# A one-layer hybrid trunk: the output projection of tile 6 spread over the last tile's inverse levels, a split last projection, and router logits from unnormalised rows

## The chip, the cores and the metric

One Trainium2 chip, one core, one launch. Times are microseconds (us) on the device for that core; one execution was also recorded by the hardware profiler. Everything is float32.

## What is computed

For 1024 tokens of width 1024, cut to what matters here:

```python
h = rms_norm(x, attn_norm_g);  proj = h @ w_in            # 1024 x 2824
y_a = gated_delta_rule(...)    # 4 heads of 128; a chunk of 64 needs the inverse of (I + strict lower)
y_a = rms_norm(o_a, gdn_out_norm_g) * silu(a_z)
y_b = swa_sink_attention(...)  # 8 heads of 64, own and previous chunk, a sink logit per head
x = x + concat([y_a, y_b]) @ w_out
tok = rms_norm(x, ffn_norm_g)
gl = tok @ w_group + b_group   # 4 groups, top 1;  el = tok @ w_expert + b_expert, top 2 of 4 experts
for e in range(16):
    gu = tok @ w_gate_up[e];  act = silu(gu[:, :256]) * gu[:, 256:]
    y = y + gates[:, e:e+1] * (act @ w_down[e])
x = x + y
```

## The kernel before

Each engine has its own program, written out by hand: PE (TensorE, matmuls and transposes), ACT (ScalarE, copies out of PSUM and exponentials), DVE (VectorE), POOL (GpSimd), SP (only starts DMAs). Semaphores join them. Each engine takes its instructions in the order of its program, so a wait holds all that stands behind it.

**First part, eight tiles of 128 tokens.** `run_tiles` calls `body(t, nx, pv, nn)` for tiles 0 to 7. Beside tile t's own recurrence and attention, the body projects tile t+1 (`nx`), finishes tile t-1 (`pv`, the "late" work) and scales and turns tile t+2 (`nn`). In the last tile, 7, `nx` is None, so the 2824-column projection that fills PE elsewhere is not there. After it `late(7)` finishes tile 7.

A body has a loop over six inverse levels. In each, PE multiplies into bank 3 (`X,aTm`), ACT copies that to `Y`, PE multiplies `Y` and the running inverse into banks 2 and 5, and DVE subtracts the results from `X` and `aTm` (the lines `L1253`, `L1261`). `xT0_ready` is the DVE's start of that chain (`L1237`).

The late work of a tile is: turn `y_mix` (PE), copy to `pT` (ACT), multiply by `wo_sb` in two halves of 512 columns (`out_half`, 8 slices k each, accumulated in one bank), add the rows of x (`add_x`, `L1162`, into `sc`, also called `xr`), square and sum (ACT), the reciprocal root in 12 small steps (`rsqrt`, `L940` to `L946`), scale to `y_mix` (`L1168`), which is also stored as `h_mid`, turn the scaled rows (`turn_hm`), copy with the gain (`L1174`, `hT2`), multiply by the router matrix (`w_rt`), add the bias (`L1179`, `lg`).

**Routing.** From `lg`, DVE finds groups and experts (`route_picks`), PE counts ranks, DVE gives each token a slot and makes one-hot rows (`row_hots`, `L1014`, `L1015`; `gate_hot`, `L1019`), PE sums them into tables in banks 0 (rows) and 3 (gates). For tiles 0 to 5 this is done ahead: `picks_ahead` in the last body, `rows_ahead` in `late(7)`. Tiles 6 and 7 follow after the last logits. `rows_ready` lets POOL gather.

**Second part, 32 expert steps.** Expert e has a first slot set (even step) and a second (odd step), each up to 128 rows, gathered from `h_mid` and scattered to `out` by POOL. Before the first step PE loads 17 flags into registers (`second`, `spilled`); an odd step's matmuls are skipped when its flag is 0. Weights stream through four ring slots, of which three lie in the memory of `w_in`, and the fourth in that of `w_out`.

## Time and profile before

| | us |
|---|---|
| three runs | 1098.81, 1102.18, 1107.79 |
| median | 1102.18 |
| profiled execution, its own time | 1106.72 |
| span that the profile shows of it | 1104.5 |
| mean granted TensorE clock of it | 0.942 |

The span runs from the first to the last recorded instruction, so 2.2 us of the profiled execution lie outside it. That execution is 4.5 us above the median, within what the three runs differ by. Every start time below counts from the start of the span. PE is recorded as busy for 90% of the span.

### The profile page before, as it was taken

The page shows a single profiled execution, that of the slowest core. Times are in us where ns is not written, and L with a number is a line of the kernel's source. Part 1 is how long each engine was busy: PE and PEld are TensorE (multiplying, and loading weights), DVE is VectorE, ACT ScalarE, POOL GpSimd, SP SyncE. Part 2 cuts the span into 40 slices and gives each one's busy share as a digit, 9 for nine tenths or more (in the row PEclk, how much of TensorE's full clock was granted, in tenths as well). Part 3 has the DMA queues.
Part 4 walks back from the last instruction along what each step waited for, and adds up shares of the span by engine and source line. Part 5 has one row for each costly group of instructions (what it writes and reads, how often), then busy time and mean ns, then how long its engine had stood idle before and what let it go on. Part 6 is the DMA issues. An engine that isn't in the chain of part 4 may idle for free.

```text
span 1104.5 us, 17185 instructions
## 1 busy us (share of the span) xinstructions
PE 997.0 (90%) x6912; PEld 690.0 (62%) x6912; DVE 591.3 (54%) x1768; ACT 215.3 (19%) x453; POOL 156.2 (14%) x227
## 2 busy tenths in 40 slices
PE   6999999999999999999999967874698998987994
PEld 2456656656656656656666655744677786866873
DVE  1446756757665675674684675575124333333332
ACT  1333233223223222321331330100000000000000
POOL 6010010010010010010010020001123223333231
PEclk9989999999999999999999978886799999989997
DMA  9700101100100100000000002804157777767321
GB/s 319 301 19 2 39 1 40 39 1 39 39 1 39 39 1 39 22 18 39 20 1 39 20 1 75 326 15 162 61 191 279 261 250 251 270 231 275 100 63 40
DMA packets 48521, 109.57 MB, mean 99 GB/s; under 512 B 10289, under 2 KB 11569, under 8 KB 48433
## 3 DMA queue, kind: packets, MB, share of 16 engines
q1 hardware_dynamic: 32880, 82.87, 21.1%
q0 software_dynamic: 13824, 25.20, 6.9%
q8 instruction: 63, 1.03, 0.4%
q10 hardware_dynamic: 1728, 0.26, 0.1%
q14 instruction: 26, 0.20, 0.1%
HBM read 108.30 MB, written 25.17 MB: 121 GB/s over the span
## 4 chain that ended last, share of the span: by engine, by line
PE 80%; DVE 10%; DMA 4%; issue 4%; ACT 1%; POOL 0%; POOLq 0%; ACTq 0%; DVEq 0%
PE pm L341 73%; PE pm L344 7%; DMA qkvT<-h_mid,w_sb 2%; DMA y_mix<-h_mid,w_sb 1%; DVE X L1253 1%; DMA sc<-h_mid,w_sb 1%; DVE y_mix L1168 0%; DVE ctmp L1230 0%; ACT ci L754 0%; DVE qkT L1241 0%; DVE aTm L1203 0%; DVE bs L946 0%; DVE bs L944 0%; DVE bs L945 0%; DMA xt<-in_x 0%
## 5 line engine op out<-in xcount | busy, mean ns | idle before, releaser
L341 PE MATMUL pm<-w_sb,hT 128*128 128x512 f32 (+1 forms) x768 | 315.8, 567 | 2.9 <-DVE hT L1074 2.8
L341 PEld LDWEIGHTS pm<-w_sb,hT 128*128 128x128 f32 x768 | 145.3, 193 | 153.5 <-issue 145.1
L341 PE MATMUL pm<-wo_sb,pT 128*128 128x512 f32 x256 | 120.7, 627 | 1.2 <-ACT pT L811 1.2
L341 PE MATMUL pm<-ctmp,w_sb 128*128 128x128 f32 x768 | 90.7, 280 | 0.0
L341 PEld LDWEIGHTS pm<-ctmp,w_sb 128*128 128x128 f32 x768 | 89.5, 197 | 0.0
L1116 DVE SCALAR_TENSOR_TENSOR pqkv<-ci,cw,pqkv 128x128 f32<-128x128 f32 x288 | 77.7, 346 | 20.5 <-ACT pqkv L759 20.0
L341 PEld LDWEIGHTS pm<-wo_sb,pT 128*128 128x128 f32 x256 | 50.3, 202 | 60.5 <-issue 58.9
L1515 POOL TENSOR_TENSOR tail<-tail,rows 128x512 f32<-128x512 f32 x8 | 10.2, 1276 | 489.1 <-ACT aTm L778 489.1
L915 ACT ACTIVATE X<-pm 128x256 f32<-128x256 f32 x32 | 12.3, 384 | 315.3 <-PE pm L341 292.4
L341 PE MATMUL pm<-w_sb,Y 128*128 128x512 f32 x152 | 70.2, 605 | 2.9 <-DVE Y L1423 2.9
L1253 DVE TENSOR_TENSOR X<-X,pm 128x256 f32<-128x256 f32 (+1 forms) x40 | 16.8, 419 | 75.3 <-PE pm L341 75.3
L344 PE MATMUL pm<-ident,y_mix 128*128 128x128 f32 x192 | 29.0, 301 | 25.3 <-DVE y_mix L1333 14.2
L341 PE MATMUL pm<-ci,w_sb 128*128 128x128 f32 x448 | 51.2, 275 | 0.0
L341 PEld LDWEIGHTS pm<-ci,w_sb 128*128 128x128 f32 x448 | 50.6, 192 | 0.0
L341 PEld LDWEIGHTS pm<-w_sb,Y 128*128 128x128 f32 x152 | 28.0, 195 | 31.2 <-issue 31.2
L1162 DVE TENSOR_TENSOR sc<-sc,pm 128x512 f32<-128x512 f32 x16 | 11.0, 688 | 66.1 <-PE pm L341 66.1
L344 PEld LDWEIGHTS pm<-ident,y_mix 128*128 128x128 f32 x192 | 24.4, 156 | 31.6 <-DVE y_mix L1333 14.5
L1433 DVE SCALAR_TENSOR_TENSOR xt<-pm,w_sb,xt 128x512 f32<-128x512 f32 x16 | 11.6, 749 | 50.6 <-PE pm L341 50.6
L1433 DVE SCALAR_TENSOR_TENSOR pqkv<-pm,w_sb,pqkv 128x512 f32<-128x512 f32 x16 | 11.6, 748 | 45.4 <-PE pm L341 45.4
L845 ACT ACTIVATE Y<-pm 128x256 f32<-128x256 f32 (+1 forms) x48 | 18.3, 382 | 86.9 <-PE pm L341 86.9
L344 PE MATMUL pm<-ident,qkvT 128*128 128x128 f32 x128 | 18.6, 293 | 18.3 <-issue 10.0
L1433 DVE SCALAR_TENSOR_TENSOR tail<-pm,w_sb,tail 128x512 f32<-128x512 f32 x16 | 12.0, 751 | 40.6 <-PE pm L341 40.6
(273 smaller groups left out, 1502.3 us busy)
## 6 DMA issues: line engine op xcount, KB each, us to landing
w_sb<-in_w_gate_up SPq DMA_DIRECT2D x12, 2048.0 KB, 10.2
w_sb<-in_w_down SPq DMA_DIRECT2D x12, 1024.0 KB, 5.9
w_sb<-in_w_in SPq DMA_DIRECT2D x5, 2048.0 KB, 17.3
wo_sb<-in_w_gate_up SPq DMA_DIRECT2D x4, 2048.0 KB, 11.2
xt<-in_x SPq DMA_DIRECT2D x8, 512.0 KB, 3.3
wo_sb<-in_w_out SPq DMA_DIRECT2D x1, 4096.0 KB, 23.1
sc<-in_x SPq DMA_DIRECT2D x8, 512.0 KB, 3.3
out<-sc SPq DMA_DIRECT2D x8, 512.0 KB, 2.6
```

The lines of the kernel that those rows point to most:

```text
L341: return pe.matmul(o_, lhsT=l_, rhs=r_, start=start, stop=stop, skip_group_check=True)
L344: return pe.transpose(o_, in_, ident[:, :])
L845: act.activation(Yd[rows_], heads(pm[3], CH)[rows_], ACT.Copy).then_inc(B.y_copied, 1)
L915: act.activation(tnh, pm[2 + p % 2][:, 0:DE], ACT.Tanh, scale=0.5).then_inc(M.tanh_ready, 1)
L1116: ins = v.scalar_tensor_tensor(cv[:, i, :], ci[:, i, j:j + P], cw[:, j, i:i + 1], cv[:, i, :], ALU.mult, ALU.add)
L1162: v.tensor_tensor(xr[:, 512 * n:512 * n + 512], xr[:, 512 * n:512 * n + 512], pm[6 + n][:, :], ALU.add).then_inc(B.xm_ready, 1)
L1253: v.tensor_tensor(Xd[rows_], Xd[rows_], heads(pm[2], CH)[rows_], ALU.subtract).then_inc(B.x_updated, 1)
L1433: ins = v.scalar_tensor_tensor(y[:, n * 512:n * 512 + 512], pm[4 + 2 * b + n][:, :], gate, y[:, n * 512:n * 512 + 512], ALU.mult, ALU.add)
L1515: g.tensor_tensor(qk_in[:, 0:QH, :], qk_in[:, 0:QH, :], gqk[:, None, 0:DH].broadcast_to([P, QH, DH]), ALU.mult)
```

## The change

Seven things are done to the program.

1. In tile 7 the late work of tile 6 is laid out over the levels. `out_half` takes a list of slices: five slices of the first half stand before level 0, three in level 0, four and four of the second half in levels 1 and 2, the turning in level 3, the logits in level 4. The results go to banks 0 and 1 instead of 6 and 7, and the attention scores of tile 7 go to `xt`, since `sc` now holds tile 6 longer. The 29 DVE instructions of `picks_ahead` are cut in four pieces, which with `add_x`, `copy_hT2`, `factor` and `scale_xm` are put behind the levels' own instructions. PE's `rank_ahead` moves behind level 5.
2. In `late(7)` the attention half of `y_mix` (slices 4 to 7) is turned and projected first, and the other half after `ya_ready`.
3. In every tile the logits are made from the unnormalised rows (`turn_xm` turns `xr`), and the row's factor is applied when the logits are copied (`scalar_tensor_tensor`). The scaled rows are still made for `h_mid`, on DVE, and in `late(7)` on ACT.
4. The last tile leaves out the update of the state `S`, which nothing reads.
5. The gates of all eight tiles are made after `rows_ready`: their 16 one-hot arrays (two picks by eight tiles) are built there one by one, where before twelve stood in `rows_ahead` and four behind `rows_ready`.
6. PE, and the other engines, load one register with all flags packed in its bits (`powers`), and an odd step tests its bit with a register operation. PE's first expert step waits for `rows_ready`, not `table_ready`.
7. SP issues the nine MB of the first three ring slots before the stores of tile 6.

```diff
+        def scores(t):
+            return sc_last if t == NT - 1 else sc
+
+        def late_banks(t):
+            return (pm[0], pm[1]) if t == NT - 2 else (pm[6], pm[7])
...
-                if pv is not None:
-                    store(pv)
...
+                if pv is not None:
+                    store(pv)
 
                 sp.wait_ge(B.p_turned, t + 1)
+                if nx is None:
+                    sp.wait_ge(L.mid_stored, 32 * t)
+                    sp.wait_ge(B.hm_turned, 2 * t)
...
+            def out_half(t, n, ks=range(KD), first=0, last=KD - 1):
+                for k in ks:
+                    ins = mm(late_banks(t)[n][:, :], yT[:, k, :], wo_sb[:, k, n * 512:(n + 1) * 512], k == first, k == last)
+                if ks[-1] == last:
+                    ins.then_inc(B.out_done, 1)
...
+            def turn_xm(t):
+
+                for n in range(2):
+                    pe.wait_ge(B.xm_ready, 2 * t + n + 1)
+                    for k in range(4):
+                        ins = turn(late_banks(t)[n][:, k * P:(k + 1) * P], xr[:, (4 * n + k) * P:(4 * n + k + 1) * P])
+                    ins.then_inc(B.hm_turned, 1)
...
-
-            def turn_hm(t):
-                pe.wait_ge(B.hm_ready, t + 1)
-                for k in range(KD):
-                    ins = turn(pm[6 + k // 4][:, (k % 4) * P:(k % 4 + 1) * P], y_mix[:, k * P:(k + 1) * P])
-                ins.then_inc(B.hm_turned, 1)
-
-            def logits(t):
-                pe.wait_ge(B.hT2_ready, 2 * t + 2)
...
+                    if k % 4 == 0:
+                        pe.wait_ge(B.hT2_ready, 2 * t + 1 + k // 4)
+                    ins = mm(late_banks(t)[0][:, 0:NL], hT2[:, k, :], w_rt[:, k, :], k == 0, k == KD - 1)
...
-                        mm(pm[3][:, 0:P], hot_mod[u], hot_gate[u], u == 0, False)
...
-                turn_y(t)
-                out_half(t, 0)
-                out_half(t, 1)
+                pe.wait_ge(B.yb_ready, t + 1)
+                for k in range(4, KD):
+                    ins = turn(pm[7][:, (k % 4) * P:(k % 4 + 1) * P], y_mix[:, k * P:(k + 1) * P])
+                ins.then_inc(B.y_turned, 1)
+                pe.wait_ge(B.yT_ready, t + 1)
+                for n in range(2):
+                    out_half(t, n, range(4, KD), 4, 3)
+                pe.wait_ge(B.ya_ready, t + 1)
+                for k in range(4):
+                    ins = turn(pm[2][:, k * P:(k + 1) * P], y_mix[:, k * P:(k + 1) * P])
+                ins.then_inc(B.y_turned, 1)
+                pe.wait_ge(B.yT_ready, t + 2)
+                for n in range(2):
+                    out_half(t, n, range(4), 4, 3)
+                turn_xm(t)
+                logits(t)
                 rows_ahead()
-                turn_hm(t)
-                logits(t)
...
+                if pv is not None and nx is not None:
+                    pe.wait_ge(B.yT_ready, pv + 1)
                     out_half(pv, 0)
...
+                if nx is None:
+                    pe.wait_ge(B.yT_ready, pv + 1)
+                    pe.wait_ge(F.chunk_copied, 6 * NT)
+                    out_half(pv, 0, range(0, 5))
+                elif pv is not None:
                     out_half(pv, 1)
                 ahead(2)
-                if nx is None:
-                    rank_ahead()
...
-                    turn_hm(pv)
+                if pv is not None and nx is not None:
+                    turn_xm(pv)
...
+                        if nx is None:
+                            out_half(pv, 0, range(5, KD))
+                        elif pv is not None:
                             logits(pv)
-                    elif l == 1 and nx is not None:
+                    if nx is None:
+                        if l == 1:
+                            out_half(pv, 1, range(0, 4))
+                        elif l == 2:
+                            out_half(pv, 1, range(4, KD))
+                        elif l == 3:
+                            turn_xm(pv)
+                        elif l == 4:
+                            logits(pv)
...
+                if nx is None:
+                    rank_ahead()
                 pe.wait_ge(B.v_ready, t + 1)
-                for h in range(H):
...
+                if nx is not None:
+                    for h in range(H):
+                        ins = mm(pm[5][:, h * P:(h + 1) * P], kd[:, h, :], V[:, h, :])
+                    ins.then_inc(B.s_done, 1)
...
-            pe.wait_ge(R.gate_hots, 1)
-            for u in late_hots:
-                ins = mm(pm[3][:, 0:P], hot_mod[u], hot_gate[u], False, u == late_hots[-1])
+            for u in range(TOPK * NT):
+                pe.wait_ge(R.gate_hots, u + 1)
+                ins = mm(pm[3][:, 0:P], hot_mod[u], hot_gate[u], u == 0, u == TOPK * NT - 1)
             ins.then_inc(R.gates_summed, 1)
...
-            second = [pe.value_load(full[0:1, e:e + 1], min_val=0, max_val=1) for e in range(NE)]
-            spilled = pe.value_load(full[0:1, NE:NE + 1], min_val=0, max_val=1)
+            spilled = pe.value_load(full[0:1, 0:1], min_val=0, max_val=2 ** (NE + 1) - 1)
...
-                with pe.If(second[ORDER[p // 2]] > 0):
+                e = ORDER[p // 2]
+                with pe.If(spilled % 2 ** (e + 1) > 2 ** e - 1):
...
-                    pe.wait_ge(R.table_ready, 1)
+                    pe.wait_ge(R.rows_ready, 1)
...
+                act.wait_ge(B.y_turned, t + 1)
+                act.activation(yT[:, 4:8, :], heads(pm[7]), ACT.Copy).then_inc(B.yT_ready, 1)
+                act.wait_ge(B.y_turned, t + 2)
+                act.activation(yT[:, 0:4, :], heads(pm[2]), ACT.Copy).then_inc(B.yT_ready, 1)
                 square_xm(t)
+                act.wait_ge(B.late_step, VL * NT)
+                act.activation(y_mix[:, :], xr, ACT.Copy, scale=bs[:, 89:90]).then_inc(B.hm_ready, 1)
...
-                v.wait_ge(A.exp_out, 1)
-                route_step(gates(0, AHEAD))
-                v.wait_ge(F.h_turned, NT)
-                v.wait_ge(F.chunk_done, 6 * NT)
                 for c in range(TOPK):
                     for t in range(AHEAD):
-                        row_hots(c, t)
-                        gate_hot(c, t).then_inc(A.hots, 1)
+                        row_hots(c, t).then_inc(A.hots, 1)
...
                     for b in range(2):
-                        v.tensor_tensor(hT2[:, 4 * b:4 * b + 4, :], heads(pm[6 + b]), wide(gain2[:, 4 * b:4 * b + 4]),
-                                        ALU.mult).then_inc(B.hT2_ready, 1)
+                        v.wait_ge(B.hm_turned, 2 * self.t + b + 1)
+                        v.tensor_tensor(hT2[:, 4 * b:4 * b + 4, :], heads(late_banks(self.t)[b]),
+                                        wide(gain2[:, 4 * b:4 * b + 4]), ALU.mult).then_inc(B.hT2_ready, 1)
...
-                    v.tensor_tensor(lg[:, bass.ds(self.t, 1), :], pm[6][:, 0:NL].unsqueeze(1), b_rt.unsqueeze(1),
-                                    ALU.add).then_inc(B.lg_ready, 1)
+                    v.scalar_tensor_tensor(lg[:, self.t, :], late_banks(self.t)[0][:, 0:NL], bs[:, 89:90], b_rt,
+                                           ALU.mult, ALU.add).then_inc(B.lg_ready, 1)
...
                 f.add_x(0)
                 f.add_x(1)
-                f.norm()
                 f.copy_hT2()
+                f.factor()
                 f.copy_logits()
...
-                if nx is None and nn is None and t == NT - 1:
-                    picks_ahead()
-                if pv:
+                if pv and nx:
                     pv.add_x(0)
                     pv.add_x(1)
...
-                    pv.norm()
+                if pv and nx:
                     pv.copy_hT2()
+                    pv.factor()
+                    pv.scale_xm()
...
+                    if not nx:
+                        if l == 1:
+                            pv.add_x(0)
+                            v.wait_ge(R.iotas, 1)
+                            route_groups(0, AHEAD)
+                        elif l == 2:
+                            pv.add_x(1)
+                        elif l == 3:
+                            pv.copy_hT2()
+                            route_first(0, AHEAD)
+                        elif l == 4:
+                            pv.factor()
+                            pv.scale_xm()
+                            route_second(0, AHEAD, A.exp_in)
+                        elif l == 5:
+                            pv.copy_logits()
+                            picks_ahead()
...
+                if nx:
+                    step(v.tensor_tensor(S[:, :, :], S[:, :, :], wide(cd), ALU.mult))
+                else:
+                    v.wait_ge(L.mid_stored, 32 * t)
...
+            tt(full_f, full_f, powers, ALU.mult)
+            step(v.tensor_reduce(gmax[:, 0:1], full_f, AX_X, ALU.add))
+            v.tensor_copy(full, gmax[:, 0:1]).then_inc(R.ready, 1)
+            v.wait_ge(R.ready, 1)
+            v.wait_ge(A.exp_out, 1)
+            v.wait_ge(R.exp_out, 1)
+            step(gates(0, NT))
+            for c in range(TOPK):
+                for t in range(NT):
+                    gate_hot(c, t).then_inc(R.gate_hots, 1)
...
+            for e in range(NE + 1):
+                step(g.memset(powers[:, e:e + 1], float(2 ** e)))
```

On PE, in the last tile from the end of its first small products to its first level, before:

```order
L341 MATMUL pm6<-wo_sb,pT 128x512 x8
L341 MATMUL pm3<-qkvT 128x128 x4
L341 MATMUL pm5<-qkvT 128x128 x4
L341 MATMUL pm7<-wo_sb,pT 128x512 x8
L341 MATMUL pm1<-w_sb,upper_strict 128x96
L341 MATMUL pm1<-w_sb,ones 128x96
L341 MATMUL pm2<-eye,aTm 64x64 x8
L344 MATMUL pm6<-ident,y_mix 128x128 x4
L344 MATMUL pm7<-ident,y_mix 128x128 x4
L341 MATMUL pm3<-X,aTm 64x64 x8
L341 MATMUL pm4<-S,qkvT 128x128 x4
L341 MATMUL pm6<-w_rt,pT 128x20 x8
```

And now (`wo_sb,pT` are slices of the output projection, `eye,aTm` turns the start of the inverse, `X,aTm` is level 0):

```order
L352 MATMUL pm3<-qkvT 128x128 x4
L352 MATMUL pm5<-qkvT 128x128 x4
L352 MATMUL pm0<-wo_sb,pT 128x512 x5
L352 MATMUL pm2<-eye,aTm 64x64 x8
L352 MATMUL pm3<-X,aTm 64x64 x8
L352 MATMUL pm4<-S,qkvT 128x128 x4
L352 MATMUL pm0<-wo_sb,pT 128x512 x3
L352 MATMUL pm2<-Y,aTm 64x64 x8
L352 MATMUL pm5<-aTm,Y 64x64 x8
L352 MATMUL pm3<-X,aTm 64x64 x8
L352 MATMUL pm1<-wo_sb,pT 128x512 x4
```

The first half's eight slices are cut in five and three, the second half begins in level 1, and the transposes, the logits and the two rank products have left this place.

On DVE, at the place where the inverse's start is made in the last tile, before (`lg` to `w_sb` is routing, the row `sc<-sc,pm6` is `add_x`, and three masked products follow it):

```order
L954 TENSOR_TENSOR w_sb<-w_sb 128x96 x2
L984 TENSOR_TENSOR w_sb<-w_sb 128x96
L1028 TENSOR_TENSOR w_sb<-w_sb 128x16 x6
L1162 TENSOR_TENSOR sc<-sc,pm6 128x512
L1162 TENSOR_TENSOR sc<-sc,pm7 128x512
L1230 TENSOR_TENSOR ctmp<-ctmp,bs 128x512
L1232 TENSOR_TENSOR Y<-pm3,ctmp 64x4x64
L1233 TENSOR_TENSOR ctmp<-pm3,ctmp 64x4x64
```

And now, where the mask of `dT` (`ctmp<-ctmp,upper`) is followed at once by the product with beta and the masked products:

```order
L1278 TENSOR_TENSOR ctmp<-ctmp,upper 128x512
L1282 TENSOR_TENSOR ctmp<-ctmp,bs 128x512
L1284 TENSOR_TENSOR Y<-pm3,ctmp 64x4x64
L1285 TENSOR_TENSOR ctmp<-pm3,ctmp 64x4x64
L1286 TENSOR_TENSOR ctmp<-pm3,ctmp 64x4x64
L1288 TENSOR_TENSOR aTm<-ctmp,level_mask 128x4x64
L1289 TENSOR_TENSOR aTm<-eye,aTm 128x4x64
```

The same engine in level 3 now has the two copies of the turned rows and part of the routing behind its own two subtractions:

```order
L1306 TENSOR_TENSOR X<-X,pm2 128x4x64
L1314 TENSOR_TENSOR aTm<-aTm,pm5 128x4x64
L1228 TENSOR_TENSOR pT<-pm0,gain2 128x512
L1228 TENSOR_TENSOR pT<-pm1,gain2 128x512
L1023 TENSOR_REDUCE w_sb<-w_sb 128x6
L1000 TENSOR_TENSOR w_sb<-w_sb 128x24 x2
L1005 TENSOR_REDUCE w_sb<-w_sb 128x6
L1000 TENSOR_TENSOR w_sb<-w_sb 128x24
```

On PE, in the late work of tile 7, before (the alternating one-hot products go on to twelve pairs, and only then come the turning and the logits):

```order
L344 MATMUL pm6<-ident,y_mix 128x128 x4
L344 MATMUL pm7<-ident,y_mix 128x128 x4
L341 MATMUL pm6<-wo_sb,pT 128x512 x8
L341 MATMUL pm7<-wo_sb,pT 128x512 x8
L341 MATMUL pm0<-pqkv,ci 128x128
L341 MATMUL pm3<-xt,ci 128x128
L341 MATMUL pm0<-pqkv,ci 128x128
L341 MATMUL pm3<-xt,ci 128x128
L341 MATMUL pm0<-pqkv,ci 128x128
L341 MATMUL pm3<-xt,ci 128x128
```

And now:

```order
L355 MATMUL pm7<-ident,y_mix 128x128 x4
L352 MATMUL pm6<-wo_sb,pT 128x512 x4
L352 MATMUL pm7<-wo_sb,pT 128x512 x4
L355 MATMUL pm2<-ident,y_mix 128x128 x4
L352 MATMUL pm6<-wo_sb,pT 128x512 x4
L352 MATMUL pm7<-wo_sb,pT 128x512 x4
L355 MATMUL pm6<-ident,sc 128x128 x4
L355 MATMUL pm7<-ident,sc 128x128 x4
L352 MATMUL pm6<-w_rt,pT 128x20 x8
L352 MATMUL pm0<-pqkv,ci 128x128 x10
```

The four-slice projection stands between the two turns of `y_mix`, and the one-hot products of tiles 0 to 5 stand behind the logits.

## Rows read from the trace of the kernel before

**Rows 1.** The page: the clock granted to TensorE, in tenths, in 40 slices.

```profile
PEclk9989999999999999999999978886799999989997
```

**Rows 2.** Waits of PE, 0 to 650 us: line waited for, sum, times, longest.

```profile
PE pm L344 <- DVE y_mix L1168: 2.5, 6, 0.4
```

**Rows 3.** Timeline of DVE, last tile: start, length, instruction, idle before.

```profile
664.78 0.18 DVE L967 TENSOR_REDUCE w_sb<-lg 128x6 f32<-128x24 f32 x1
...
671.20 0.68 DVE L1162 TENSOR_TENSOR sc<-sc,pm 128x512 f32<-128x512 f32 x1
...
676.41 0.69 DVE L1162 TENSOR_TENSOR sc<-sc,pm 128x512 f32<-128x512 f32 x1 [4.53 <-PE pm L341]
...
679.42 0.42 DVE L1237 TENSOR_TENSOR aTm<-eye,aTm 128x256 f32<-128x256 f32 x1
...
706.53 0.41 DVE L1253 TENSOR_TENSOR X<-X,pm 64x256 f32<-64x256 f32 x1 [1.60 <-PE pm L341]
...
713.99 0.69 DVE L1303 TENSOR_TENSOR V<-pm,bs 128x512 f32<-128x512 f32 x1 [1.75 <-PE pm L341]
...
715.82 0.76 DVE L1317 TENSOR_TENSOR y_mix<-pm,bs 128x256 f32<-128x256 f32 x2
...
723.08 0.69 DVE L1333 TENSOR_TENSOR y_mix<-X,gsz 128x512 f32<-128x512 f32 x1
```

**Rows 4.** Timeline of PE, last tile and late work.

```profile
658.39 9.33 PE L341 MATMUL pm<-wo_sb,pT 128*128 128x512 f32 x16
...
669.34 7.03 PE L341 MATMUL pm<-wo_sb,pT 128*128 128x512 f32 x16
...
684.26 1.97 PE L344 MATMUL pm<-ident,y_mix 128*128 128x128 f32 x8 [3.25 <-DVE y_mix L1168]
...
689.08 3.44 PE L341 MATMUL pm<-w_rt,pT 128*128 128x20 f32 x16
...
726.97 16.05 PE L341 MATMUL pm<-wo_sb,pT 128*128 128x512 f32 x32 [1.17 <-ACT pT L811]
```

**Rows 5.** Timeline of PE in tile 5, a level's product.

```profile
515.07 0.68 PE L341 MATMUL pm<-X,aTm 64*64 64x64 f32 x16
```

**Rows 6.** Timeline of DVE in the late work of tile 7.

```profile
723.69 0.25 DVE L954 TENSOR_TENSOR w_sb<-w_sb 128x96 f32<-128x96 f32 x1
...
728.22 0.28 DVE L1014 TENSOR_SCALAR ci<-w_sb 128x128 f32<-128x128 f32 x1
...
736.72 0.69 DVE L1162 TENSOR_TENSOR sc<-sc,pm 128x512 f32<-128x512 f32 x1
...
743.05 0.69 DVE L1162 TENSOR_TENSOR sc<-sc,pm 128x512 f32<-128x512 f32 x1 [5.64 <-PE pm L341]
...
749.28 1.29 DVE L1174 TENSOR_TENSOR pT<-pm,gain 128x512 f32<-128x512 f32 x2 [1.26 <-PE pm L344]
...
753.40 0.18 DVE L1179 TENSOR_TENSOR lg<-pm,rows 128x20 f32<-128x20 f32 x1 [2.83 <-PE pm L341]
```

**Rows 7.** Timeline of DVE, end of the routing.

```profile
761.95 0.29 DVE L1014 TENSOR_SCALAR ci<-w_sb 128x128 f32<-128x128 f32 x1
...
763.76 0.16 DVE L1050 TENSOR_REDUCE w_sb<-w_sb 128x2 f32<-128x8 f32 x1
...
766.86 0.18 DVE L1352 CAST w_sb<-w_sb 128x32 int32<-128x32 f32 x1
...
768.45 0.18 DVE L1377 CAST w_sb<-w_sb 128x17 int32<-128x17 f32 x1
```

**Rows 8.** Timeline of PE, the first expert step's transposes.

```profile
780.21 1.94 PE L344 MATMUL pm<-ident,qkvT 128*128 128x128 f32 x8 [10.02 <-issue]
```

**Rows 9.** The chain that ended last: start, length, what.

```profile
768.01 4.71 DMA qkvT<-h_mid,w_sb
```

**Rows 10.** Windows: length, PE, PEld, DVE, ACT, POOL busy (x), clock, DMA, GB/s.

```profile
688.00:690.00 2.00, 2.00 (x12) 2.00 (x11) 0.00 (x0) 0.00 (x0) 0.00 (x0) 0.50 0.99 332
728.00:730.00 2.00, 2.00 (x4) 0.97 (x3) 1.95 (x9) 0.00 (x0) 0.00 (x0) 0.50 0.00 0
```

122 lines of the change are left out of this document (57 added, 65 removed).

## The prediction

> **What bounds the kernel now.** The page comes first. TensorE holds nearly its full clock (2.4 GHz) nearly everywhere and loses it in one stretch, slices 24 to 29, which is 635 to 800 us [rows 1]. Before that place PE works almost without a gap, so what counts there is PE's own work; after it PE works through the experts with few waits. In between no engine is the bound: PE and DVE hand work to each other, and every microsecond of that chain moves the end. I therefore read the waits of PE before 650, then the timelines of DVE and PE from 650 to 790, then the granted clock in windows. All times below are on the axis of the profiled execution.
>
> **Tiles 1 to 6: minus 2.5 us.** In each of these bodies PE waits 0.4 us for the scaled rows, 2.5 in all [rows 2]. The turning now needs only `xr`, which is ready much earlier, so this goes. DVE does copies first and then 12 steps and the scaling. Between the turning and level 0's subtraction PE has, at full clock, a level's product 0.6 [rows 5], keys by state 1.05, the logits 1.8 (half of the 3.44 at half clock [rows 4]) and a second product 0.6, with the hand-over some 4.4 us; DVE's copies (1.29 [rows 6]), 12 steps (2.3) and scaling (0.75) take 4.35, so they just fit. The later store of `h_mid` is 4 us behind and nobody needs it for two levels. I count no cost, and up to 0.5 us a tile (3 us) for the bound.
>
> **Start of the inverse in tile 7: minus 12.2 us.** DVE is at 664.78 when it turns to the ahead routing, 6.4 us until 671.20; then it adds x for the first half, then waits 4.53 for PE's second half and adds at 676.41, and makes the inverse's start at 679.42, done at 679.84 [rows 3]. The masked products take from the end of the adding, 677.10, to there, 2.8 us. Without routing and adding they stand right behind 664.78: done at 667.6. Their inputs are early enough: the key products, which stood behind the first half of the projection, now come right at 658.4, where the first half began [rows 4], on the half clock, and end near 663. Five slices (ten of the sixteen passes of a half, 7.03 us at full clock [rows 4], so 4.4) fit into the rest. What is late next is this DVE chain itself, not PE.
>
> **The levels: about 0.** From the inverse's start to the subtraction of level 4 it is 679.84 to 706.53, 26.7 us [rows 3], with a 3.25 us wait for the scaled rows and then work on the half clock [rows 4, 10]. Now PE keeps its full clock, since it goes on working, but carries eleven more slices (22 passes of 0.44, 9.7 us). A product of the level is 0.6 us from start to start [rows 5]; three of them, DVE's subtraction and the hand-over, 0.5, stand in the chain. Level by level: turning and copying the start 1.2; level 0 with its product 0.6, keys by state 1.05, three slices 2.64, product 0.6, ends at 673.7; level 1 adds 0.5 + 0.6 + 3.5 + 0.6, 678.9; level 2 the same with 0.8 for the turns, 684.9; then scores and their maximum as before, 4.75 from level to level, 689.7, which hides the turning (1.04); level 4 has copies (1.3) and the logits' second half in the chain and takes 3.95, where the old one took 2.35. The subtraction of level 4 falls at 693.7, against 706.53: still 12.8 us ahead. DVE's inserted pieces are under PE's: adding and group routing (0.7 + 1.9) under the four slices of level 2, the first picks (1.1) under the logits.
>
> **The queues that are passed: 0.** On SP the weights of three ring slots now come before the stores of tile 6; they start when the last projection is done and have two levels' more time than the stores ask for, so nothing waits behind them; the x rows of tile 7 wait for those stores and are wanted only by the late work. POOL's 17 small fills stand before a signal that DVE needs only in level 1. If either were late, its price would be DVE's wait in the last tile, and I take none.
>
> **From level 4 to the logits of tile 7: minus 15.** Call the subtraction of level 4 T. Before, the logits are written at 753.58, T + 47.05 [rows 6]. Now, behind T: 1.3 for the inverse's own subtractions, factor 2.3, scaling 0.75, second picks 1.4, so level 5's product comes at T + 5.8 and its end at T + 6.9; the old order had T + 5.7. V's product needs PE's 1.1 and then `copy_logits` and the last picks (2.1) to pass: T + 9.1, against T + 7.46 [rows 3]. That is the price of this step, 1.6 us, and the missing state update pays 1.3 of it: the recurrence's half is in `y_mix` at T + 17.6 (was T + 17.24), the attention's half at T + 11.0. PE turns and copies that (1.3) and works 7.0 us on half of the projection, T + 19.3 at full clock; then turns the other half, copy 0.6, 7.0 more: T + 27.5. Before, the whole of it started at T + 20.4 and took 16.05 [rows 4], to T + 36.5. DVE meanwhile routes (3.7 + 12 pairs of arrays at 0.45, the rate of 761.95 to 763.76 [rows 7]; the triples ran from 728.22 to 736.72 [rows 6]) until T + 26.8, just ahead of PE. Adding ends at T + 28.2; then turning the second half 0.5, copying 0.7, logits 0.93 on one side, squares 1.25 and twelve steps 2.35 on the other: T + 32.1. The old chain took 743.74 to 753.58, 9.8 us [rows 6], the new one 3.9. Together 47.05 minus 32.1, 15.0.
>
> **The clock's surcharge: plus 2.** PE idled 7 us before the last projection, was then at 0.50 [rows 10], and 16.05 us went where 14.06 would do at full clock. Now it idles less but still has gaps from T + 4 to T + 12, so I expect the same surcharge of 2; the bounds are 0 and 7, the latter for all of the first half at 1.2 GHz. The Trainium skill (TensorE: Matmul & The Clock Gate, "Part 1: The HAM clock gate (the "warmup" mystery)") says that a model should leave the ramp out, as under 1% of a typical span. By that rule the sum would be 2 us better; the rows show the ramp as 2 us in this one place.
>
> **Routing tail: 0.** From the logits to `rows_ready` it is 753.58 to 767.04 [rows 6, 7], 13.5 us of the same instructions.
>
> **From there to the experts: minus 5.9.** Before, PE begins the first turn at 780.21, 13.2 us after `rows_ready`, after 10.02 without a releaser [rows 8]. The gather had landed at 772.72 [rows 9]. What stands in PE's program in that gap is 17 register loads, 0.59 each. Now: flags 0.66 as before plus 0.45, gates 0.8, 16 arrays at 0.25 are 4.1, last product 0.4, one load 0.6, hand-overs 0.3: 7.3. The gather needs 5.7 and is under it. POOL's first base gathers wait for the gates, 1.6 later than before, and are wanted over 20 us later. The Trainium skill (DMA: Bandwidth & Descriptors, "Latency and other measured facts") puts the floor of a `tensor_load` at some 600 ns; 17 of them give 10.2, and one load 0.6, so the sum stays, and its rule speaks against the rival that the stop is a fixed one.
>
> **Experts: 0.** Loads of the later weights follow PE's progress, the fourth ring slot is loaded 30 us before it is used, and PE's waits for gathers come from POOL's order of steps.
>
> **The sum.** 2.5 + 12.2 + 0.6 + 15.0 + 5.9 are 36.2, less 2 for the clock, 34. From the profiled execution's 1106.7 that is 1072.7; it stood 4.5 above the median of the runs, so against the median of 1102.2 it is 1068.
>
> **Rivals.**
> The stop before the experts is not the number of loads: then 10 us stay behind the gates instead of 0.6, and the gain falls by 9.4, to 1077. For it: no row names the loads. Against: nothing else is in the program there.
> DVE's pieces are not under PE's: if route pieces and late work add to every level (up to 8 us of the 12 put in) and PE drops to half clock in the first half (7 instead of 2), the gain is 21 to 28: 1074 to 1081. For it: levels 3 to 5 have little PE work; against: the pieces are shorter than the slices beside them.
> Nothing arrives: the experts' part ends when something of its own rhythm ends, and the gain dies there, 1092 to 1102. For it would be that PE waits several times for gathers; against, that these are sequential with the first step.
> Slower: the flag test. An odd step now makes a register operation with a remainder in PE's queue, 16 times, in front of a turn that the next copies wait for. By the nearest row, a register load of 0.59, it is 9.4 us, time 1077; it turns the sign when one costs over 2.1 us, and at 3 it gives 1116. No row shows such an operation; against a high price is only that it touches no memory.
> Better: the routing tail runs at full clock and the levels hide more, 1050 to 1058.
>
> **Chances.** The forecast 0.73 (its own range 1058 to 1078), the fixed stop 0.05, exposed pieces 0.12, nothing arrives 0.04, slower 0.03, better 0.03. What a measurement of this kernel can tell from no change is about 1%, 11 us. Faster by over 1% is all but the last part of "nothing arrives" and "slower": 0.93; within 1% 0.04; slower 0.03. The range from 1056 to 1083 takes in the forecast's bounds, the fixed stop and the exposed pieces.
>
> **What would show it.** In the profile after: the start of the inverse (`aTm<-eye,aTm`) some 12 us nearer to the masked `dT`, with no wait of DVE between; PE's clock at 1.0 through levels 0 to 2; the logits of tile 7 about 28 us earlier; at most 8 us from `rows_ready` to the first turn; PE's busy time in the experts' part unchanged. I am wrong if the gap before the first turn stays near 10 us, if the odd steps show an idle time that was not there, or if the levels in the last tile take clearly more than 27 us.

## Result and profile after

The changed kernel takes 1073.98 us (median of 4 runs, 1067.81 to 1075.96) against 1102.06 (4 runs, 1098.81 to 1107.79), a ratio of 0.9725, 95% interval 0.9687 to 0.9764. It was run twice more beside other kernels: 1072.85 (6 runs, ratio 0.9727, 0.9685 to 0.9769) and 1069.44 (6 runs, 0.9680, 0.9648 to 0.9711). The median of all 16 is 1072.55, which is 29.7 below 1102.2. The forecast was 1068, a gain of 34.

The first profiled execution of the changed kernel took 1075.61, span 1073.8. Its clock row, in slices of 26.8 us, answers to [rows 1]:

```profile
PEclk9999999999999999999999996986999998988998
```

Between 635 and 800 us three digits are below 9 (slices 25, 27 and 28) where six were. PE's waits up to 650 us (engine, output and line, what is waited for: us in total, times, longest):

```profile
PE pm L355 <- DVE xt L1118: 9.0, 1, 9.0
PE pm L352 <- DVE hT L1126: 2.8, 2, 1.4
PE pm L355 <- ACT ci L794: 2.4, 7, 0.3
PE pm L352 <- DVE V L1374: 0.8, 1, 0.8
```

The wait for the scaled rows [rows 2] is gone. Now DVE in the last tile (start, duration, engine, line, operation; it answers to [rows 3] and [rows 6]; `L1306` is the subtraction of level 4, the `L1214` row ends the last adding, `lg` are the logits of tile 7, and `CAST ... 128x32` is the end of `rows_ready`, as in [rows 7]):

```profile
667.13 0.68 DVE L1278 TENSOR_TENSOR ctmp<-ctmp,upper 128x512 f32<-128x512 f32 x1
670.25 0.42 DVE L1289 TENSOR_TENSOR aTm<-eye,aTm 128x256 f32<-128x256 f32 x1
...
697.45 0.41 DVE L1306 TENSOR_TENSOR X<-X,pm 64x256 f32<-64x256 f32 x1 [1.47 <-PE pm L352]
...
706.68 0.68 DVE L1374 TENSOR_TENSOR V<-pm,bs 128x512 f32<-128x512 f32 x1
714.62 0.69 DVE L1408 TENSOR_TENSOR y_mix<-X,gsz 128x512 f32<-128x512 f32 x1
...
725.35 0.69 DVE L1214 TENSOR_TENSOR sc<-sc,pm 128x512 f32<-128x512 f32 x1 [0.32 <-PE pm L352]
...
729.70 0.24 DVE L1233 SCALAR_TENSOR_TENSOR lg<-pm,bs,rows 128x20 f32<-128x20 f32 x1
...
743.15 0.18 DVE L1427 CAST w_sb<-w_sb 128x32 int32<-128x32 f32 x1
```

From the masked `dT` to the inverse's start it is 3.1 us, and DVE waits for nothing in between. From the end of the last adding to the logits it is 3.9 us (726.04 to 729.94), where it was 9.8 [rows 6]. PE, answering to [rows 4] and [rows 8]:

```profile
709.92 7.13 PE L352 MATMUL pm<-wo_sb,pT 128*128 128x512 f32 x16 [0.69 <-ACT pT L860]
718.18 7.13 PE L352 MATMUL pm<-wo_sb,pT 128*128 128x512 f32 x16 [0.69 <-ACT pT L862]
...
745.61 3.79 PE L352 MATMUL pm<-xt,ci 128*128 128x128 f32 x16 [3.26 <-DVE xt L1077]
749.19 1.91 PE L352 MATMUL pm<-hT,ci 128*128 128x128 f32 x8
750.89 1.20 PE L352 MATMUL pm<-hT,w_sb 128*128 128x128 f32 x8
751.93 1.04 PE L355 MATMUL pm<-ident,qkvT 128*128 128x128 f32 x8
```

Both halves of the last projection go at full clock, 7.13 us each. In front of the first turn (the last row) stand no longer 10 us without a releaser, but products: those of the 16 gate arrays, 745.61 to 752.09, the first of them at half clock (the granted clock from 743.3 to 752 was 0.55). The windows of the last tile (length, busy time of PE, PEld, DVE, ACT, POOL, granted clock, DMA share, GB/s):

```profile
646.00:664.00 18.00, 11.93 (x53) 11.11 (x54) 13.91 (x47) 6.34 (x11) 6.52 (x32) 0.50 0.97 368
664.00:697.00 33.00, 30.86 (x344) 20.73 (x345) 20.70 (x64) 5.64 (x14) 0.00 (x0) 0.97 0.05 18
697.00:703.00 6.00, 6.00 (x48) 5.66 (x47) 4.57 (x21) 1.47 (x3) 0.00 (x0) 0.50 0.01 1
703.00:734.00 31.00, 25.63 (x147) 16.16 (x145) 27.84 (x115) 3.98 (x7) 0.00 (x0) 0.99 0.22 73
```

The levels, which ran at half clock in part [rows 10], now have 0.97.

**One table for all runs.** Tiles 1 to 6 scatter from one execution to the next (below), so I cut each profiled execution at the same events. A: from the start to PE's turn of tile 7's rows (`ident,qkvT`, the first behind 640). B: to the inverse's start. C: to the subtraction of level 4. D: to the logits of tile 7. E: to the end of the row numbers' cast. F: to the first expert turn. G: to the end. "Lost" is the clock that was not granted between 60 and 640, the sum over windows of 2 us of 2 times (1 minus granted clock), which is worked out and no row. All in us.

```
kernel             A  (lost)    B     C     D     E     F      G    B to G   ratio
before          650.6 (6.1)   28.9  27.1  46.9  13.6  13.2  324.3   453.9
packed_only     648.0 (5.1)   29.9  24.8  45.3  13.6   5.9  325.1   444.6   0.9920
after           652.4 (11.1)  17.8  27.2  32.3  13.6   8.6  321.9   421.4   0.9725
control_after   646.0 (5.1)   17.8  27.7  32.3  13.0   8.4  321.5   420.6   0.9727
control_again   652.5 (11.1)  17.8  27.2  32.3  13.6   8.6  321.4   420.9   0.9680
loads17         646.0 (5.1)   17.8  27.7  32.3  13.0  17.2  326.3   434.3   0.9808
gates_in_gap    649.1 (8.5)   17.8  27.9  32.3  13.0   5.8  323.5   420.3   0.9680
whole_projection 646.7 (5.3)  17.8  27.1  42.8  13.6   8.6  321.6   431.4   0.9821
picks_first     645.8 (5.1)   24.2  28.8  30.5  13.6   8.5  321.8   427.4   0.9769
slices_first    646.7 (5.2)   17.8  28.7  32.3  13.0   8.3  321.5   421.5   0.9696
stores_first    648.8 (8.5)   16.6  27.2  41.9  13.1   7.6  320.4   426.7   0.9801
x_then_weights  646.7 (5.2)   17.8  27.1  32.3  13.6   8.7  321.6   421.1   0.9723
pieces_early    649.8 (8.0)   17.8  27.3  31.4  13.3   7.6  320.7   418.1   0.9667
pieces_gates    649.0 (8.5)   16.6  27.2  30.1  13.0   5.7  320.9   413.5   0.9678
```

The changed kernel's own three executions agree in B to G within 0.8 us, while A differs by 6.5. So a stage tells differences of about 1 us, while the three medians of this one program (4, 6 and 6 runs) differ by 4.5. But this was tried only on the changed kernel: the kernel before and `packed_only`, whose code is the same up to the end of E but for 17 small fills on POOL, differ by 1.0, 2.3 and 1.6 in B, C and D, with the clock.

### The profile page after: what moved, and what is told of

Read it like the earlier page. It is cut to its first block, busy times and chain, and to the rows that moved or that the text cites. A ratio compares the mean times of both kernels' runs of the same rounds, so it can differ in the third digit from the quotient of the medians.

```text
span 1073.8 us, 17149 instructions
## 1 busy us (share of the span) xinstructions
PE 993.0 (92%) x6904; PEld 686.4 (64%) x6904; DVE 588.6 (55%) x1763; ACT 216.7 (20%) x454; POOL 157.8 (15%) x244
## 4 chain that ended last, share of the span: by engine, by line
PE 84%; DVE 7%; DMA 5%; issue 2%; ACT 1%; POOL 0%; POOLq 0%; DVEq 0%; ACTq 0%
PE pm L352 77%; PE pm L355 6%; DMA qkvT<-h_mid,w_sb 2%; DMA y_mix<-h_mid,w_sb 1%; DVE X L1306 1%; DMA sc<-h_mid,w_sb 1%; ACT ci L794 0%; DVE w_sb L1000 0%; DMA xt<-in_x 0%; POOL out L1664 0%; DVE hT L1126 0%; DVE Y L1504 0%; DVE X L1502 0%; DVE tail L1514 0%; DVE bs L990 0%
## 5 line engine op out<-in xcount | busy, mean ns | idle before, releaser
L1306 DVE TENSOR_TENSOR X<-X,pm 128x256 f32<-128x256 f32 (+1 forms) x40 | 16.8, 419 | 63.6 <-PE pm L352 63.6
L1214 DVE TENSOR_TENSOR sc<-sc,pm 128x512 f32<-128x512 f32 x16 | 11.0, 686 | 59.7 <-PE pm L352 59.7
L788 ACT ACTIVATE tail<-pm 128x512 f32<-128x512 f32 (+1 forms) x24 | 12.7, 529 | 100.3 <-PE pm L352 100.3
L1514 DVE SCALAR_TENSOR_TENSOR hT<-pm,w_sb,hT 128x512 f32<-128x512 f32 x16 | 12.0, 751 | 37.5 <-PE pm L352 37.5
L352 PEld LDWEIGHTS pm<-Y,aTm 64*64 64x64 f32 x576 | 22.0, 135 | 15.2 <-issue 13.6
```

Of the source, the lines that this page charges most:

```text
L352: return pe.matmul(o_, lhsT=l_, rhs=r_, start=start, stop=stop, skip_group_check=True)
L788: act.activation(dst, pm[BANK[c]][:, 0:n], ACT.Copy).then_inc(F.chunk_copied, 1)
L1214: v.tensor_tensor(xr[:, 512 * n:512 * n + 512], xr[:, 512 * n:512 * n + 512], late_banks(self.t)[n][:, :], ALU.add).then_inc(B.xm_ready, 1)
L1306: v.tensor_tensor(Xd[rows_], Xd[rows_], heads(pm[2], CH)[rows_], ALU.subtract).then_inc(B.x_updated, 1)
L1514: ins = v.scalar_tensor_tensor(y[:, n * 512:n * 512 + 512], pm[4 + 2 * b + n][:, :], gate, y[:, n * 512:n * 512 + 512], ALU.mult, ALU.add)
```

## Experiments

**The changed kernel again (`control_after`, `control_again`).** No edit.

> The changed kernel itself, once more, beside the kernel before. It tells two things. First the ratio of the times: 0.97 to 0.98 is expected. Second, where the granted clock dips to 0.50 in tiles 1 to 6, inside continuous work: in the first profiled execution of this kernel that was four times or more and the recurrence of tile 6 began 2.35 us later than in the kernel before, although the waits for the scaled rows were gone. Theory: the dips are not a property of the changed code, they fall elsewhere in another execution of the same kernel, and bodies without a dip take the same 84.1 us. Rival: the changed rhythm itself costs them; then the same bodies (those with a dip at 150, 234, 406 and 490) dip again, and the inverse's start of tile 7 lies at 670 within half a microsecond.

> The changed kernel once more, on the chip of the other three, so that differences of 2 to 3 us can be judged. Expected: 0.970 to 0.975 of the kernel before. Its trace should once more have the same times from the turn of tile 7's rows to the logits within 0.5 us, wherever the clock dipped in the tiles before.

The rival of the first fell as it was stated: in `control_after` tile 7's turn is 6.4 us earlier, and there are three dips (314, 399, 570) instead of those at 80, 150, 235, 406 and 491. But `control_again` dips at the very places of the first profiled execution. The same program thus has at least two patterns of dips.

The dips are not scattered over the work. Every tile's body has, ahead of its large products, a run of small ones; the last of these is, in one body of the profile after:

```profile
403.90 1.93 PE L352 MATMUL pm<-ones,ctmp 128*128 128x1 f32 x16
```

From the first body's small products to 640, every dip in all 14 profiles begins between 0.5 us before the end of these products and 2.2 us behind it, read in windows of 0.5 us. What differs from one execution to another is only which of the bodies get one. Here are the dip behind the row above, and a body of the same execution without a dip, whose small products end at 321.7 (columns as above):

```profile
406.00:408.00 2.00, 2.00 (x4) 0.86 (x3) 1.93 (x9) 0.00 (x1) 0.00 (x0) 0.61 0.00 0
408.00:410.00 2.00, 2.00 (x3) 0.68 (x3) 1.66 (x11) 0.73 (x2) 0.00 (x0) 0.54 0.00 0
```

```profile
320.00:322.00 2.00, 2.00 (x17) 1.82 (x17) 1.73 (x8) 0.00 (x0) 0.00 (x0) 1.00 0.00 0
322.00:324.00 2.00, 2.00 (x6) 0.95 (x5) 1.90 (x10) 0.15 (x1) 0.00 (x0) 1.00 0.00 0
```

In `control_after` the body of the first dip has one too, only 6.4 us earlier, since its small products end at 399.4:

```profile
398.00:400.00 2.00, 2.00 (x14) 1.68 (x15) 1.79 (x8) 0.00 (x0) 0.00 (x0) 0.85 0.04 8
400.00:402.00 2.00, 2.00 (x4) 0.76 (x3) 1.86 (x10) 0.41 (x1) 0.00 (x0) 0.50 0.00 0
402.00:404.00 2.00, 2.00 (x5) 0.84 (x4) 1.66 (x11) 0.32 (x2) 0.00 (x0) 0.80 0.00 0
```

PE is recorded as busy throughout in these windows; the dip at 406 loses 2 times 0.39 and 2 times 0.46, 1.7 us. A minus "lost" is 641.3, 640.9 and 641.4 in the three executions. What picks the bodies is open, and no run changed the small products, so that these bring the dips about is not shown either.

**The flags taken apart again (`loads17`), and packed alone (`packed_only`).** The first is the changed kernel with

```diff
-            spilled = pe.value_load(full[0:1, 0:1], min_val=0, max_val=2 ** (NE + 1) - 1)
+            second = [pe.value_load(full[0:1, e:e + 1], min_val=0, max_val=1) for e in range(NE)]
+            spilled = pe.value_load(full[0:1, NE:NE + 1], min_val=0, max_val=1)
...
-                with pe.If(spilled % 2 ** (e + 1) > 2 ** e - 1):
+                with pe.If(second[e] > 0):
```

and the second is the kernel before with the opposite edit and nothing else of the change.

> The changed kernel with the one packed number of flags taken apart again: PE loads 17 registers before the experts and the odd steps test a register against zero, with no remainder; the two DVE instructions that packed the flags go. Theory: 17 loads at 0.59 are 10.0 us and one is 0.6, so the first turn comes later than now; the gates' products no longer matter (they end with the loads or before), so from the cast of the row numbers to the first turn it is some 16 us instead of 8.6, or, if the loads run while the gates are made, 13.2 as in the kernel before; the time rises by 5 to 8 us. Rival: the stop is a fixed one, then the gap stays within 1 us of 8.6. The same run prices the flag test: if a remainder in the odd steps cost what a load costs (16 times 0.59, 9.4 us), the experts' part would be that much shorter here than 321.9; expected is no difference.

> The kernel before with the packed flags alone. Theory: the first turn is then set by the gather that landed at 772.72 (or by the gates' products, whichever is later) instead of by the loads at 780.21, so the time falls by 6 to 8 us; what the clock gives back at the first products may add 1 to 2. The sum of the prediction gave this part 5.9. Rival, the fixed stop: 0. Rival, a price of the odd steps' tests: the gain at the first turn is lost again behind it.

Measured: `loads17` 1081.65 (ratio 0.9808, interval 0.9749 to 0.9867); `packed_only` 1094.37 (0.9920, 0.9882 to 0.9958), 7.9 below before. PE around the first turn in `loads17` and then in `packed_only`:

```profile
743.93 1.14 PE L352 MATMUL pm<-hT,w_sb 128*128 128x128 f32 x8
753.99 1.94 PE L355 MATMUL pm<-ident,qkvT 128*128 128x128 f32 x8 [8.92 <-issue]
```

```profile
763.73 1.06 PE L341 MATMUL pm<-hT,w_sb 128*128 128x128 f32 x4
767.54 1.94 PE L344 MATMUL pm<-ident,qkvT 128*128 128x128 f32 x8 [2.75 <-DMA qkvT<-h_mid,w_sb]
```

The stop of [rows 8] comes back with the 17 loads (F 17.2 against 8.4, 8.8 more) and goes with them (5.9 against 13.2, 7.3 less); what is late next in the kernel before is the gather. 8.83 us for 16 further loads is 0.55 each. The fixed stop has fallen. The Trainium skill (DMA: Bandwidth & Descriptors, "Latency and other measured facts") has some 600 ns as the floor of a `tensor_load`; the trace's 0.55 us is 8% under it.

The flag tests have no price that shows beyond 0.8 us for 16 of them. With them G is 325.1 in `packed_only` and 324.3 in the kernel before; `loads17`, without them, has 326.3, the changed kernel 321.5. What does change G is the clock of the first step: its first turn takes 1.94 at half and 1.04 at full clock. In the 36 us from the first turn on, 3.6 to 4.6 of clock are lost in the three kernels with G over 324, and none in the others. The expectation that G would not differ was wrong by this: a stop before the experts costs its own length and 3 to 5 us more in the step behind it. By the stages the flags are thus worth 13.7 us (B to G) inside the change; the medians, 1081.65 against 1072.85, show 8.8.

**The last projection in one piece (`whole_projection`).**

```diff
-                pe.wait_ge(B.yb_ready, t + 1)
...
-                for n in range(2):
-                    out_half(t, n, range(4), 4, 3)
+                turn_y(t)
                 pe.wait_ge(B.yT_ready, t + 1)
+                out_half(t, 0)
+                out_half(t, 1)
                 turn_xm(t)
```

and ACT copies the turned `y_mix` whole.

> The changed kernel with one part undone: tile 7's output projection is one piece again, turned and copied whole when both halves of y_mix are there, instead of half of it going ahead under DVE's routing arrays. The rest of the change stays. Theory: the second half of y_mix ends some 8 us after the first is turned, and the 7.1 us of the first half now stand behind it, so the logits of tile 7 come 7 us later (32.1 behind level 4's subtraction become 39), and PE, which idles some 9 us before the projection, may start it at half clock, 1 to 2 more: time 7 to 9 us above the changed kernel. Rival: DVE's routing arrays, not PE, set the adding; then the projection's first half was in their shade and undoing it costs only the part that sticks out, under 3 us.

Measured 1082.34 (0.9821, 0.9762 to 0.9880), 9.8 above the median of all runs of the changed kernel, and D 42.8 against 32.3:

```profile
713.77 16.19 PE L352 MATMUL pm<-wo_sb,pT 128*128 128x512 f32 x32 [1.17 <-ACT pT L841]
```

The whole takes 16.2 us, where the two halves were 14.3: the clock's surcharge of 2 that the kernel before had. So the split is worth its 7.1 us and, beside that, 3.4 of clock and hand-over. DVE's arrays didn't set the adding; the rival fell. By the medians this is the largest single part that was tried; by the stages the flags are.

**All ahead routing before the inverse's start (`picks_first`).**

```diff
+                if not nx:
+                    v.wait_ge(R.iotas, 1)
+                    route_groups(0, AHEAD)
+                    route_first(0, AHEAD)
+                    route_second(0, AHEAD, A.exp_in)
+                    picks_ahead()
                 step(v.tensor_tensor(aT[:, :, :], dT[:, :, :], wide(beta), ALU.mult))
```

with the four pieces between the levels removed.

> The changed kernel with one part undone: DVE makes all of the ahead routing (groups, first and second picks, last picks; 6.4 us in the kernel before) in one piece before the inverse's start in tile 7, as before, instead of in four pieces between the levels. Theory: the start of the inverse comes 6.4 us later and the levels get back what the pieces cost them, which the prediction held to be 1.6 us behind level 4 and nothing before; the time rises by 4 to 6 us. Rival: the pieces are not under PE's slices but stand in the chain of the levels (up to 6.4 us in all); then the levels shorten by nearly as much, and the time stays within 1.5 us.

Measured 1075.17 (0.9769, 0.9702 to 0.9835). B is 24.2 against 17.8, the 6.4 of the routing; D is 30.5 against 32.3, the 1.8 that the second and last picks cost behind level 4 (the prediction had 1.6); C is 28.8 against 27.2 to 27.7, so the levels are longer without the pieces, not shorter. The clock is at least part of it: it was 0.55 in the first 6 us from the inverse's start, where the changed kernel had 1.00. Together 6.4 in B to G; the median shows 2.6 of it, within its scatter.

**All slices before level 0 (`slices_first`).**

```diff
-                    out_half(pv, 0, range(0, 5))
+                    out_half(pv, 0)
+                    out_half(pv, 1)
...
-                        if nx is None:
-                            out_half(pv, 0, range(5, KD))
```

and the same for levels 1 and 2.

> The changed kernel with one part undone: all sixteen slices of tile 6's output projection stand before level 0, as before, and none lies between the levels. Theory: PE then sets the first level's start, eleven slices of 0.88 at full clock, 9.7 us, later; the levels 0 to 2, whose slices were 3, 4 and 4, shorten by as much as the slices exceed the hand-overs to DVE, some 5 to 6 us; what is left, 3 to 5 us, is the time in which PE idles for DVE in the levels. Less filled levels should also show half clock in the levels, 1 to 2 us more. So 4 to 7 us above the changed kernel. Rival: the slices between the levels lie in the chain in full, and only their place changes: then 0 to 1.

Measured 1070.06 (0.9696, 0.9639 to 0.9752), not slower: C is 28.7 against 27.2 to 27.7, 1.0 to 1.5 more, and nothing else moves. My theory fell and the rival held: between the levels the slices stand in PE's chain in full. PE's row in front of the levels, x32 instead of x10:

```profile
659.91 14.06 PE L352 MATMUL pm<-wo_sb,pT 128*128 128x512 f32 x32
```

Laying the slices out between the levels, the most elaborate piece of the change, is worth about 1 us. The prediction's level by level sum had them in the chain, which was right; I did not draw the conclusion from it.

**SyncE's order (`stores_first`, `x_then_weights`).** In the first the two blocks change places, in the second the weights go behind the x rows:

```diff
+                if pv is not None:
+                    store(pv)
                 if nx is None:
                     sp.wait_ge(F.chunk_done, 6 * NT)
                     for i in range(RING - 1):
                         load_gate_up(i)
                         load_down(i)
-                if pv is not None:
-                    store(pv)
```

> The changed kernel with one part undone: SyncE's queue takes the stores of tile 6 ahead of the weights of three ring slots again. Theory: no wait hangs on either order, since the weights are wanted 80 us later and the stores' rows a whole tile later; the time stays within what the runs scatter (under 0.4%), and the weights' transfers move behind level 0 to 5. Rival: the weights then collide with the gathers and the last stores, and the first experts wait: 2 us or more.

> The changed kernel with SyncE's queue in the order: stores of tile 6, x rows of tile 7, weights of three ring slots. It tells what the 8.5 us wait was worth that appeared in the run with the stores and then the weights ahead of the x rows. Theory: the x rows were late only because they stood behind 9 MB of weights in one queue; in front of them they land in 3 us, no wait appears, the logits of tile 7 come 25.2 us behind those of tile 6 as in the changed kernel, and the time is the changed kernel's within the scatter. Rival: the weights at that time, 700 to 723, take the transfers' share from what the last tile needs (stores, first gather) wherever they stand; then 2 us or more remain.

`stores_first` took 1080.03 (0.9801, 0.9740 to 0.9862), against my theory of no effect, and not by the rival's reason either: the experts' stage G is 320.4, not longer. SyncE's queue, and the instruction of DVE that waited:

```profile
697.32 0.32 SPq L303 DMA_DIRECT2D h_mid<-y_mix  x1
...
705.82 9.74 SPq L296 DMA_DIRECT2D w_sb<-in_w_down  x1
715.68 1.12 SPq L320 DMA_DIRECT2D sc<-in_x  x1
```

```profile
728.08 1.28 DVE L1214 TENSOR_TENSOR sc<-sc,pm 128x512 f32<-128x512 f32 x2 [8.53 <-DMA sc<-in_x]
```

The x rows of tile 7 stand behind nine MB of weights, are issued at 715.68, which is 66.9 us behind tile 7's turn against 53.0 in `control_after` (698.99), and land at 728. D grows by 9.6; B and G happen to be 1 shorter each, so B to G is 5.7 longer. In `x_then_weights` (1072.93, 0.9723, 0.9689 to 0.9757) no stage differs from the changed kernel by more than 0.1 outside the 0.6 by which its own executions differ, with the same weights moving at the same late time. So it is the place in the queue, not the transfers' load. In the kernel before the same order did no harm only because the last adding came some 20 us later (x rows issued at 709.86, first used at 736.72): this part of the change gains nothing by itself and protects 8.5 us of the others.

**The gates in a gap (`gates_in_gap`), the pieces earlier (`pieces_early`), and both (`pieces_gates`).** The first moves `step(gates(0, NT))` and 5 of the 16 arrays ahead of `v.wait_ge(R.rows_summed, 1)`, with the two waits that stood before them. The second:

```diff
+                if not nx:
+                    v.wait_ge(R.iotas, 1)
+                    route_groups(0, AHEAD)
                 for l in range(len(LEVELS)):
...
                             pv.add_x(0)
-                            v.wait_ge(R.iotas, 1)
-                            route_groups(0, AHEAD)
+                            route_second(0, AHEAD, A.exp_in)
...
                             pv.copy_hT2()
-                            route_first(0, AHEAD)
+                            picks_ahead()
...
+                            route_first(0, AHEAD)
```

where the last line stands in level 0, behind `r_ready`.

> The changed kernel with the gates and 5 of the 16 gate arrays moved into the 2.2 us in which DVE waits for the summed rows, ahead of the cast of the row numbers. In the changed kernel the first turn waits for the last gate product, at half clock, 3 us behind the landing of the first gather. Theory: the pieces fit into the wait, the gates' products end some 3 us earlier, the first turn is set by the gather's landing at 5.7 behind the cast, and the time falls by 2 to 3 us. Rival: the pieces are longer than the wait (gates 0.8 and 5 times 0.25 are 2.05, against 2.16) and delay the cast and the gather; then the gain is 1 or nothing. Second rival: what follows (base gathers, the first gating) is next, and the gain at the first turn is lost within two steps.

> The changed kernel with DVE's pieces of ahead routing put elsewhere, nothing else: the groups before level 0 (DVE waits 4.8 us there for PE), the first picks behind level 0 (2.6 us of waiting), the second behind level 1 (2.6) and the last picks behind level 3 in place of the first picks (2.0). So none of the 3.5 us of routing stands any more behind level 4, where DVE has no wait at all from the level's subtraction to the end of its routing arrays. Theory: this stretch is DVE's own chain; V comes when PE's product is there, 2.3 us earlier, with the levels as long as before, and the logits of tile 7 come 2 to 2.5 us earlier behind level 4's subtraction (32.25 become about 30); the time falls by about 2. Rival: PE's turns of the scores, state product and V's product set V, then under 0.8 is gained. Second rival: in the levels the pieces stick out, and what is gained behind level 4 is lost before it.

> Both together: the routing pieces early, and the gates with 5 of their 16 arrays in DVE's wait for the summed rows. The two places are independent. Theory: the first turn comes 2.6 us earlier behind the logits, as in the run with the gates alone, and 2 to 2.5 from the pieces; of the gates' part the experts gave back 2 in that run, so the time is 2.5 to 4.5 below the changed kernel. Rival: the experts' part is paced by its gathers and weights from the moment of the row numbers, then nothing is added to what the pieces give.

`gates_in_gap`: 1070.49 (0.9680, 0.9638 to 0.9723). F falls from 8.4 to 5.8, and the gather ends the wait:

```profile
745.86 1.06 PE L356 MATMUL pm<-ident,qkvT 128*128 128x128 f32 x8 [1.23 <-DMA qkvT<-h_mid,w_sb]
```

G rises by 1.6 to 2.1, so B to G is only 0.3 to 1.1 lower, as its second rival had it: PE's waits for gathers add up to 19.2 us there against 16.4 in `control_after`, and only 1.2 of them stand at the first turn. `pieces_early`: 1068.49 (0.9667, 0.9639 to 0.9695). D falls by 0.8, not 2 to 2.5, and DVE, which had no wait here, waits for PE:

```profile
700.07 0.69 DVE L1312 TENSOR_TENSOR X<-pm,bs 128x512 f32<-128x512 f32 x1 [0.41 <-PE pm L352]
701.07 0.42 DVE L1322 TENSOR_SCALAR XT<-pm 64x256 f32<-64x256 f32 x1 [0.31 <-PE pm L352]
703.24 0.69 DVE L1376 TENSOR_TENSOR V<-pm,bs 128x512 f32<-128x512 f32 x1 [1.61 <-PE pm L352]
```

PE is at half clock for the first 4 us behind level 4 there. In `pieces_gates` that stretch has 0.66, and D falls by 2.1. So DVE's chain is the bound by 0.8 us at half clock and by some 2 at a higher one: the rival was right for the half clock. `pieces_gates`: 1066.95 (0.9678, 0.9642 to 0.9713), B to G 413.5, the least of all, 7.5 below the mean of the changed kernel's three executions, of which 1.2 in B touch no edited code (PE's product of `upper` and `fs` took 1.16 us there, at full clock, and 2.08 in the profile after; `stores_first` has the same). Beside `control_again`, which was measured with them (0.9680), the times don't tell either of the two from the changed kernel; only the stages do, from one execution each. A gain of 3 to 5 us is likely but not shown.

## Why the prediction was right, and by how much not

The forecast of faster was right, and 1068 is 4.6 below the median of all runs, 6 below the first. Its sum was 34 on the profiled execution. The terms, from the stages of before and the three executions of after:

- Tiles 1 to 6, minus 2.5: A less what the clock lost is 644.5 and 642.9 (`packed_only`) without the change, and 640.3 to 641.8 with it, 2.6 less by the means. Right; but a dip more or less is 1.7, and the profile after was 1.9 us later in A than before.
- Start of the inverse, minus 12.2: B fell by 11.1 (12.1 against `packed_only`). The routing is 6.4 of it. Right within 1; it was the small products at half clock, 646 to 664, for which DVE waited 1.1 us.
- Levels, minus 0.6: plus 0.1 to 0.6 against before, 2.4 to 2.9 against `packed_only`. The old levels had 0.50 of the clock for 13 us (684 to 697) in the profile that I had, and in another execution of the same code 0.64 in 683 to 690 and 1.00 from there. Mis-sized by 0.7 to 3.5.
- Level 4 to the logits, minus 15.0: minus 14.6 (13.0 against `packed_only`). The logits are done at T + 32.5 against a forecast T + 32.1, the price of the picks is 1.8 against 1.6. The split of the projection gives 10.5 of this stage, as its run shows; of the rest, the 5.9 us less between the last adding and the logits come from two things together, the turning of the unnormalised rows and the one-hot products moved behind, and no run parts the two.
- Clock's surcharge, plus 2: not there with the projection split, 1.9 there when it is whole.
- Routing tail, 0: 0 or minus 0.6, by the clock (0.66 and 0.76 in that stage).
- `rows_ready` to the first turn, minus 5.9: minus 4.6 to 4.8. The loads gave 7.3, as the rows had it; the gates, all behind the cast now, took back 2.5 to 2.7, since their 16 products run at half clock in part (3.79 us and 1.91, in the rows above) and I had DVE's arrays as the chain.
- Experts, 0: minus 2.4 to 2.9. The first step starts at full clock, since PE comes to it from products and no longer from a stop.
- Queues, 0: right for the order as it was made, and wrong as reasoning. I said of the x rows only that they wait for the stores; that the old order would have put them behind nine MB was not looked for.

Behind A the terms add up to 31.7, and B to G fell by 32.5 to 33.3. That this is so close is partly luck: the start, the levels, level 4 to the logits and the first turn were put too high, by 1.1, 0.7 to 1.2, 0.4 and 1.1 to 1.3, and the clock's surcharge and the experts made up for them, by 2 and 2.4 to 2.9. On its own axis the forecast was 1072.7, and the three profiled executions took 1075.61, 1068.30 and 1075.15, in the mean 1073.0.

What was off is the last step, 4.5 us taken off the total because the profile before stood so far above its median. That holds only if its slow stretches lie outside the code that the change shortens. `packed_only` runs the same code in B to D in 2.9 us less (1.0 more in B, 2.3 and 1.6 less in C and D), so part of the 4.5 was probably counted twice, once in the gain and once in what was taken off. This is one execution against one, an argument and not shown; the rest of the 4.6 is within the scatter of the medians.

Of the signs that the prediction named, the start of the inverse and the clock of the levels (0.97) came as said. The gap before the first turn was to be at most 8 us and is 8.4 to 8.6. The logits of tile 7 were to come about 28 us earlier: they come 23.7 earlier in the first profile and 29.6 in `control_after`, apart by the dips in A.

Of the rivals, the fixed stop is excluded, and so is a price of the flag tests near the 9.4 us that it took (0.8 shows). The exposed pieces show only as the 1.8 us behind level 4. That nothing arrives is excluded too, though `gates_in_gap` shows it on a small scale: what comes out ahead of the first turn without a better clock is handed back to the gathers.

## What to carry to other kernels

Cut every profiled execution at the same events and compare stages: here a stage repeats within 0.6 us while the total moves by 7. Where the one profile of before is slower than the median, its slow stretches are likely to be in the very places that look worth changing, so take terms from there at less than their length. When work behind a queued load comes earlier, look up what the load itself stands behind. And undo the parts one by one: the split of the last projection (10.5 by the stages), the packed flags (13.7 by the stages and 8.8 by the medians with the rest of the change; alone 6.5 in the stages behind the cast, 7.9 by the medians) and the routing off the inverse's start (6) carry the gain, and the slices between the levels give 1. The unnormalised rows, the missing state update and the gates' new place (items 3, 4 and 5) were not undone by themselves.
